# Seven-product pairs of steps in three feed-forward stages: four back-to-back pairs instead of three spaced ones, and two of a pair's weight sums made ahead in DRAM

## The reference

```
def swiglu(x, w_gu, w_down):
    gate, up = jnp.split(x @ w_gu, 2, axis=-1)       # w_gu: 1024 x 5632
    return (jax.nn.silu(gate) * up) @ w_down         # w_down: 2816 x 1024
# x = x + 0.5 * swiglu(rms_norm(x, g), w_gu, w_down)   four times; the fifth without the 0.5
```

## Time and profile before

| | |
|---|---|
| time, median of 3 runs | 1301.13 us (1301.01 to 1303.16) |
| the profiled execution | 1300.3 us, its span 1298.3 us |
| PE busy | 99% of the span |
| DVE, ACT busy | 72%, 62% |
| DMA | 265.83 MB, mean 205 GB/s |

### The profile page before, as it was taken

How to read it: one execution, slowest core, us unless ns; L and a number is a source line. 1 busy time by engine, 2 the same in 40 slices (tenths; PEclk the granted TensorE clock), 3 DMA queues, 4 the chain that set the end, 5 groups by cost and what they waited for, 6 DMA issues and landing times.

```text
span 1298.3 us, 17145 instructions
## 1 busy us (share of the span) xinstructions
PE 1281.1 (99%) x6976; PEld 1071.9 (83%) x6976; DVE 934.5 (72%) x1091; ACT 801.0 (62%) x1046; POOL 39.8 (3%) x61
## 2 busy tenths in 40 slices
PE   7999999999999999999999999999999999999998
PEld 6888888888988888888787888888888898788887
DVE  5887777777567877866353557678878798688785
ACT  7576658766556665684443466576556757755653
POOL 0000000000000000000000000001000000000000
PEclk9999999999999999999999999999999999999999
DMA  9987635432159778455444532498893534689761
GB/s 354 294 322 227 231 125 195 163 111 87 48 209 339 233 262 290 171 214 202 147 167 146 194 127 73 169 356 260 256 319 103 206 132 151 265 232 328 231 219 33
DMA packets 40206, 265.83 MB, mean 205 GB/s; under 512 B 4476, under 2 KB 6780, under 8 KB 9152
## 3 DMA queue, kind: packets, MB, share of 16 engines
q1 hardware_dynamic: 31056, 205.71, 42.4%
q0 software_dynamic: 7920, 56.37, 16.3%
q10 hardware_dynamic: 1152, 2.66, 0.6%
HBM read 263.67 MB, written 2.11 MB: 205 GB/s over the span
## 4 chain that ended last, share of the span: by engine, by line
PE 95%; ACT 2%; DVE 2%; issue 1%; DMA 0%; SPq 0%; ACTq 0%; DVEq 0%
PE ps L2451 25%; PE ps L2452 25%; PE ps L2453 25%; PE ps L2366 8%; PE ps L2602 1%; PE ps L2377 1%; PE ps L2492 1%; PE ps L2484 1%; PE ps L2497 1%; PE ps L485 1%; PE ps L2507 1%; PE ps L487 1%; PE ps L486 1%; ACT w_hi_part L584 1%; PE ps L2424 1%
## 5 line engine op out<-in xcount | busy, mean ns | idle before, releaser
L1492 DVE TENSOR_TENSOR w_lo_part<-w_raw,w_hi_part 128x2048 fp32r<-128x2048 f32 (+2 forms) x160 | 361.3, 2262 | 135.3 <-ACT w_hi_part L584 135.3
L584 ACT ACTIVATE w_hi_part<-w_raw 128x2048 fp32r<-128x2048 f32 (+2 forms) x159 | 301.4, 1896 | 156.2 <-PE ps L2453 135.1
L2451 PE MATMUL ps<-w_hi_part,x_hi 128*128 128x512 f32 (+1 forms) x800 | 312.3, 390 | 0.8 <-DVE w_lo_part L1492 0.5
L2453 PE MATMUL ps<-w_hi_part,x_lo 128*128 128x512 f32 (+1 forms) x800 | 305.5, 382 | 0.0
L2452 PE MATMUL ps<-w_lo_part,x_hi 128*128 128x512 f32 (+1 forms) x800 | 304.8, 381 | 0.0
L584 ACT ACTIVATE w_hi_part<-arena 128x2048 fp32r<-128x2048 f32 x72 | 138.1, 1918 | 97.4 <-PE ps L2453 93.1
L1492 DVE TENSOR_TENSOR w_lo_part<-arena,w_hi_part 128x2048 fp32r<-128x2048 f32 x72 | 164.6, 2288 | 39.4 <-ACT w_hi_part L584 39.4
L2451 PE MATMUL ps<-w_hi_part,h_hi_part 128*128 128x512 f32 x464 | 186.7, 402 | 0.1
L2453 PE MATMUL ps<-w_hi_part,h_lo_part 128*128 128x512 f32 x464 | 181.4, 391 | 0.0
L2452 PE MATMUL ps<-w_lo_part,h_hi_part 128*128 128x512 f32 x464 | 181.0, 390 | 0.0
L2453 PEld LDWEIGHTS ps<-w_hi_part,x_lo 128*128 128x128 f32 x800 | 150.4, 188 | 29.8
(11 more groups left out here) (443 smaller groups left out, 1555.9 us busy)
## 6 DMA issues: line engine op xcount, KB each, us to landing
w_raw<-in_tiles SPq DMA_DIRECT2D x155, 1024.0 KB, 4.9
arena<-in_tiles SPq DMA_DIRECT2D x36, 1024.0 KB, 6.4
arena<-in_tiles POOLq DMA_DIRECT2D x24, 1024.0 KB, 9.6
t<-in_tiles POOLq DMA_DIRECT2D x18, 1024.0 KB, 10.3
mem_kv<-in_tiles POOLq DMA_DIRECT2D x6, 1024.0 KB, 10.4
w_raw<-in_tiles SPq DMA_DIRECT2D x3, 512.0 KB, 5.9
arena<-in_w_ukv POOLq DMA_DIRECT2D x1, 1536.0 KB, 14.3
arena<-in_w_dkv POOLq DMA_DIRECT2D x1, 1280.0 KB, 8.7
```

The lines of the kernel that those rows point to most:

```text
L584: nc.scalar.activation(WH[:, n % RING, 0:w], source(n), ACT.Copy).then_inc(S["w_hi"], 1)
L1492: nc.vector.tensor_tensor(WL[:, n % RING, 0:w], source(n), WH[:, n % RING, 0:w], ALU.subtract).then_inc(S["w_split"], 1)
L2451: nc.tensor.matmul(o, a_hi, w_hi, start=start, stop=False, skip_group_check=True)
L2453: return nc.tensor.matmul(o, a_lo, w_hi, start=False, stop=stop, skip_group_check=True)
```

## The change

ffn1, ffn3 and ffn4 leave `PAIRED` for a new list `QUADS`; ffn0 and ffn2 stay. In a stage of QUADS steps 0, 1, 2 are plain, and pairs (3,4), (5,6), (7,8), (9,10) follow with nothing between them. A pair's order on PE is p5, m2, m1, p3, m6, d, m7, d, m4, with the downs of the pair before. The operands of m1, m2 and p3 come through the ring of raw tiles. T1 and T3 are made in a DRAM tensor `made_sums`: SP copies the first addend there (24 copies of 1 MB, DRAM to DRAM: one after the load of each of ain's tiles 4 to 11 for ffn1, two after each of mem's four loads for ffn3, one after every third load of ffn2 for ffn4), and POOL adds the second to it with accumulating DMAs (8 for each stage: ffn1's when all its 8 copies have landed, and each not before the split of one of ain's tiles 6 to 13; ffn3's during ffn2, ffn4's during in2). SP loads the finished sums into SBUF (TA twice, TC once). DVE still makes T2, in place; T4 is made by one accumulating DMA from POOL onto T2. ACT does the norm of such a stage ahead of its first two `w_hi`.

```diff
-PAIRED = ("ffn0", "ffn1", "ffn3", "ffn4")
+PAIRED = ("ffn0",)
+QUADS = ("ffn1", "ffn3", "ffn4")
+QUAD_STEPS = (3, 5, 7, 9)
+def quad_order():
+    order = [("g0", 0), ("g1", 0), ("g0", 1), ("g1", 1), ("d", 0), ("g0", 2), ("g1", 2)]
+    for s in QUAD_STEPS:
+        order += [("p5", s), ("m2", s), ("m1", s), ("p3", s), ("m6", s), ("d", s - 2), ("m7", s), ("d", s - 1), ("m4", s)]
+    return order + [("d", 10), ("d", 9)]
...
+            def copies_after(n):
+                t = n - tile0["ain"] - 4
+                if 0 <= t < 8:
+                    return range(t, t + 1)
+                t = n - tile0["mem"]
+                if 0 <= t < 4:
+                    return range(8 + 2 * t, 10 + 2 * t)
+                t = n - tile0["ffn2"] - 4
+                if 0 <= t < 24 and t % 3 == 0:
+                    return range(16 + t // 3, 17 + t // 3)
+                return ()
+            def copy_block(i):
+                q, k = divmod(i, 2)
+                name, s = QUADS[q // len(QUAD_STEPS)], QUAD_STEPS[q % len(QUAD_STEPS)]
+                t = stored0[name] + stored_at("g0", s + k)
+                sp.dma_start(made[q, k, :, :], d["tiles"][t, :, :], max_dma_last_dim=4 * TILE).then_inc(copied(name), 16)
+            def t_load(name, s, k):
+                dst, (sem, _) = ((TA[QUAD_STEPS.index(s) % 2], t1_loaded(name, s)), (TC, t3_loaded(name, s)))[k]
+                sp.dma_start(dst, made[quad_no(name, s), k, :, :]).then_inc(sem, 16)
...
                 sp.dma_start(RAW[:, r % RING, 0:w], d["tiles"][t, :, 0:w]).then_inc(w_loaded[r % RING], 16)
+                for c in copies_after(n):
+                    copy_block(c)
...
+                def quad_of_steps(s):
+                    if s == QUAD_STEPS[0]:
+                        pe.wait_ge(S["sums"], sum_no[name, "s_lo", 0])
+                    s_product("p5", s, 7, True, False)
+                    turn_pair(s - 1 if s == QUAD_STEPS[0] else s - 2)
+                    x_product("m2", s, 5, 0, 1, True, True)
+                    if s > QUAD_STEPS[0]:
+                        turn_pair(s - 1)
+                    x_product("m1", s, 4, 0, 0, True, False)
+                    pe.wait_ge(S["snap"], snaps_to(name, s, 1))
+                    s_product("p3", s, 7, False, True)
+                    pe.wait_ge(S["sums"], sum_no[name, "c11", s])
+                    s_product("m6", s, 4, False, False)
+                    down_half(s - 2, 0)
+                    down_half(s - 2, 1)
+                    pe.wait_ge(S["sums"], sum_no[name, "c12", s])
+                    s_product("m7", s, 4, False, False)
+                    down_half(s - 1, 0)
+                    down_half(s - 1, 1)
+                    if s == QUAD_STEPS[-1]:
+                        turn_pair(10)
+                    pe.wait_ge(S["sums"], sum_no[name, "c22", s])
+                    x_product("m4", s, 4, 1, 1, False, True)
...
+            def make_sums(name, paced):
+                pool.wait_ge(copied(name), 16 * (n_pairs + (3 if name == "ffn3" else 2) * len(QUAD_STEPS)))
+                for i, n in enumerate(paced):
+                    s, k = QUAD_STEPS[i // 2], i % 2
+                    pool.wait_ge(S["w_split"], n + 1)
+                    pool.dma_start(made[quad_no(name, s), k, :, :], stored(name, ("g0", "g1")[k], s + 1), accum_op=ALU.add,
+                                   max_dma_last_dim=4 * TILE).then_inc(S["base_loaded"], 16)
+            def t4_sums(name):
+                for s in QUAD_STEPS:
+                    split(name, "m6", s)
+                    pool.dma_start(TA[QUAD_STEPS.index(s) % 2], stored(name, "g1", s), accum_op=ALU.add).then_inc(t4_added(name, s)[0], 16)
...
             for s in PAIR_STEPS:
                 pair_sums("ffn0", s)
-            for s in PAIR_STEPS:
-                pair_sums("ffn1", s)
-            pool.wait_ge(S["tile_used"], unit_of["ffn1", "p3", PAIR_STEPS[-1]] + 1)
+            make_sums("ffn1", range(tile0["ain"] + 6, tile0["ain"] + 14))
+            t4_sums("ffn1")
...
+            make_sums("ffn3", range(tile0["ffn2"] + 2, tile0["ffn2"] + 26, 3))
...
+            pool.wait_ge(*made_all("ffn3"))
+            make_sums("ffn4", range(tile0["in2"] + 1, tile0["in2"] + 9))
+            t4_sums("ffn4")
```

More of the change, by code:

```diff
@@ L824, in paired_ffn, with quad_ffn, at, x_blocks @@
                 hidden_hi(10)
+                w_hi(ends[name] + 1)
+            def quad_ffn(f, name, first):
+                def at(kind, s):
+                    return unit_of[name, kind, s]
+                def x_blocks():
+                    act.wait_ge(S["act_ready"], 4 * version[name] + 4)
+                    for half in range(2):
+                        for k in range(4):
+                            last = nc.scalar.activation(AF[:, 2 * half:2 * half + 2, k, :], PS[:, half:4:2, k * P:(k + 1) * P],
+                                                        ACT.Copy, scale=gain(name, 4 * half + k))
+                    last.then_inc(S["x_blocks"], 1)
+                def s_hi():
+                    act.wait_ge(S["sums"], sum_no[name, "s", 0])
+                    nc.scalar.activation(SH[:, :, :, :], AF, ACT.Copy).then_inc(S["x_blocks"], 1)
+                def gate(s, tb):
+                    if tb == 0:
+                        act.wait_ge(S["gu_ps"], gu_no[name, s] + 1)
+                    else:
+                        act.wait_ge(S["tile_used"], at("g1", s) + 1)
+                    if s == 0 and tb == 0:
+                        act.wait_ge(S["norm_rs"], scale_no[name] + 1)
+                    if s == 1:
+                        act.wait_ge(S["h_raw"], TB * STEPS * f + tb + 1)
+                    nc.scalar.activation(SG[:, tb, :], bank(gu_bank(s, tb), CW), ACT.Silu,
+                                         scale=RSV[:, tb:tb + 1]).then_inc(S["sg_ready"], 1)
+                def snap(dst, b, kind, s):
+                    act.wait_ge(S["tile_used"], at(kind, s) + 1)
+                    if kind == "p5" and s > QUAD_STEPS[0]:
+                        act.wait_ge(S["h_raw"], hiddens_to(f, s - 1, 1))
+                    nc.scalar.activation(dst, bank(b), ACT.Copy).then_inc(S["snap"], 1)
+                def gate_of(block, s, which, tb):
+                    act.wait_ge(S["sums"], sum_no[name, which, s])
+                    nc.scalar.activation(block[:, 0:CW], block[:, 0:CW], ACT.Silu, scale=RSV[:, tb:tb + 1]).then_inc(S["sg_ready"], 1)
+                def gate_21(s):
+                    act.wait_ge(S["tile_used"], at("m4", s) + 1)
+                    nc.scalar.activation(SG[:, 1, :], bank(4, CW), ACT.Silu, scale=RSV[:, 1:2]).then_inc(S["sg_ready"], 1)
+                def hidden_hi(s):
+                    act.wait_ge(S["ht_ps"], turns_to(f, s))
+                    nc.scalar.activation(HH[:, 2 * (s % 2):2 * (s % 2) + 2, :], pairs(bank(6)), ACT.Copy).then_inc(S["h_hi"], 1)
+                for u in range(4):
+                    turned_hi(name, u)
+                first()
+                w_hi(at("g0", 1))
+                w_hi(at("g1", 1))
+                gate(0, 0)
+                gate(0, 1)
+                x_blocks()
+                hidden_hi(0)
+                w_hi(at("d", 0))
+                w_hi(at("g0", 2))
+                gate(1, 0)
+                gate(1, 1)
+                w_hi(at("g1", 2))
+                hidden_hi(1)
+                s_hi()
+                w_hi(at("p5", 3))
+                w_hi(at("m2", 3))
+                gate(2, 0)
+                gate(2, 1)
+                w_hi(at("m1", 3))
+                snap(P5F, 7, "p5", 3)
+                w_hi(at("p3", 3))
+                w_hi(at("m6", 3))
+                hidden_hi(2)
+                snap(C11F, 5, "m2", 3)
+                w_hi(at("d", 1))
+                w_hi(at("m7", 3))
+                snap(C12F, 7, "p3", 3)
+                gate_of(C11F, 3, "c11", 0)
+                w_hi(at("d", 2))
+                gate_of(C12F, 3, "c12", 0)
+                w_hi(at("m4", 3))
+                w_hi(at("p5", 5))
+                gate_of(P5F, 3, "c22", 1)
+                w_hi(at("m2", 5))
+                gate_21(3)
+                w_hi(at("m1", 5))
+                hidden_hi(3)
+                w_hi(at("p3", 5))
+                w_hi(at("m6", 5))
+                snap(P5F, 7, "p5", 5)
+                snap(C11F, 5, "m2", 5)
+                w_hi(at("d", 3))
+                snap(C12F, 7, "p3", 5)
+                hidden_hi(4)
+                w_hi(at("m7", 5))
+                gate_of(C11F, 5, "c11", 0)
+                w_hi(at("d", 4))
+                gate_of(C12F, 5, "c12", 0)
+                w_hi(at("m4", 5))
+                w_hi(at("p5", 7))
+                gate_of(P5F, 5, "c22", 1)
+                w_hi(at("m2", 7))
+                gate_21(5)
+                w_hi(at("m1", 7))
+                hidden_hi(5)
+                w_hi(at("p3", 7))
+                w_hi(at("m6", 7))
+                snap(P5F, 7, "p5", 7)
+                snap(C11F, 5, "m2", 7)
+                w_hi(at("d", 5))
```

(57 more changed lines are left out.)

274 lines of the change are left out of this document (247 added, 27 removed).

## The result

The changed kernel takes 1314.86 us (median of 6 runs, 1311.27 to 1317.37), the kernel before 1302.65 us in the same session (6 runs, 1301.01 to 1304.52). The ratio is 1.009, with a 95% interval from 1.0072 to 1.0108: slower by 0.9%, a forecast of 1305.4 inside its range, 9.5 us too low.

The account below looks back on a forecast made before the run. The prediction took PE's work, busy 99% of the span, as the bound. From 1300.3 us, -6.9 (matmuls) +0.5 (pair waits) +9.7 (solve stall) +1.0 (in2) gave 1304.6; 0.8 for the median gave 1305.4, range 1293.5 to 1323.

Parts of the forecast that it names:

- What PE loses and gains: In the three changed stages, fewer matmuls save PE 2.3 us each, 6.9 in all; waits in the pairs add 0.5.
- The mechanism of the stall: In the triangular solve, copies and sums delay raw tiles; ACT waits in order, holding copies PE needs: 9.7 us.
- Its size and its place: Stall of 9.7 us at out0 0, landing at 326.3 us; waits at mem 2 and mem 3 counted as the same lateness.
- The copy: DRAM to DRAM copy of 1 MB in ain and mem: 3.2 us of DMA engine work, bounds 2.44 and 4.5.
- The bias_rows row: Profile row at 884 to 889 us, nearest neighbour for the copy's price: 3.0 us of work over some 4.5 us.
- the prediction's formula at out0 0: In the solve, out0 0 lands at 235.9 + 16c + 8a, c per copy, a per sum; stall is that plus 2.8 less 319.4.
- rival B: DMAs partly hidden in the solve: copy between 2.5 and 3.1 us, stall 3 to 8 us, 1298 to 1303.5 us; chance 0.13.
- The accumulation into DRAM: Each 1 MB sum into DRAM takes 4.9 us of DMA engine work, as into SBUF, bounds 2.44 and 6.
- in2: In stage in2, sums starting with ring loads at the same split make in2 7 late: +1.0 us, between 0 and 2.5.
- A: DMAs hidden in the solve: ACT meets no late tile, only the gain is left, 1294.7 us; chance 0.34.
- C: Copy takes its clock time, 4.5 us: out0 0 lands at 347, stall of 30 us in the solve, 1326 us; chance 0.11.
- D: DVE becomes the bound in the changed stages: twelve pairs lose 1 us each, DMAs hidden, 1306.7 us; chance 0.04.

Follow-up runs that it names:

- e3: The changed kernel without any copies or sums in DRAM, T1 and T3 loaded as plain stored tiles: 1296.01 us, 0.9958 of the kernel before.
- e2: The changed kernel with ffn3's eight copies behind the loads of out0's four tiles instead of mem's: 1298.6 us, 0.9971 of the kernel before.
- e4: The changed kernel with ffn1's sums waiting for mem's tile 3 split and ffn4's sums in bin instead of in2: 1295.41 us, 0.9948 of before.
- e1: The changed kernel with ffn1's eight sums waiting for the split of mem's tile 3, all copies unmoved: 1298.64 us, 0.997 of the kernel before.
- e6: The changed kernel with ffn1's eight accumulations into DRAM replaced by plain copies of the same size and places: 1298.81 us, 0.9982 of before.

## Why the prediction was right, and where not

**What PE loses and gains: right.** Forecast -6.9 us with +0.5 of waits in the pairs, -6.4; measured -2.21 - 2.04 - 2.37 = -6.6. e3, with no DRAM work, has the same stages (177.54, 177.79, 177.56). T4's accumulation does end late for ACT (three waits in ffn1, of 3.3 us at 454.65 and up to 4.9), but PE doesn't wait for it here; that margin is thin, as the prediction said, and e2 and e4 overstep it by 0.7 to 1.0 us. Of the forecast's 0.5 us for waits the stages leave 0.3.

**ffn2 at 0: right** (207.39 against 207.35).

**The mechanism of the stall: right.** Full engines from the sums' start at 243.2 us (forecast 243.1) on, ACT behind a tile of w_raw, the triangular solve's copies behind the split, PE idle; parity of bytes between the queues while both have work, 8.39 to 8.93 MB; all taken back by e1, e2 and e6. One link was missing: at mem 2 the last copy is not ACT's but DVE's, behind DVE's own split, which costs 2.5 us more than ACT's (316.0 to 313.5). At out0 0, where the prediction looked, DVE's split stands behind that copy in the kernel before (321.36, the copy at 315.52), so there ACT's is the link.

**Its size and its place: the step that failed.** Forecast 9.7 us at out0 0, measured 15.1 at mem 2. The prediction called the waits at mem 2 and mem 3 "the same lateness, not more" and priced only the last tile. But the sums are all past before mem 2: up to its landing the engines have five loads, four copies and eight sums from 243.1 on. Even with the prediction's own prices, 243.1 + 12.2 + 12.8 + 38.1 + 2.4 = 308.6 (38.1 is 39.2 less the 1.1 done). ACT wanted it at 294.40, and could have it 2.0 us late, since DVE came to its split of mem 2 only at 298.35, 2.0 us after ACT's had ended (it was 310.81 - 0.84 - 294.40 = 15.6 late, for 13.6 at PE). That is 12 us where out0 0 gave 9.7. A tile in the middle can be the worst when what pushes it back ends before it; each tile needs its own sum.

**The copy: over-priced, 3.2 instead of 2.5 us.** In ain, with a full queue, the copies of 209.28 and 218.37 landed 12.6 and 13.3 us after issue, at 221.88 and 231.67: two loads and two copies in 9.8 us, 4.9 for a load and a copy together; less 2.44 for the load, 2.5. Windows of the kernel after, q1 alone, with that full queue and then behind it:

```profile
216.90:236.60 19.70, 19.70 (x110) 16.98 (x109) 14.79 (x30) 14.32 (x24) 0.00 (x0) 1.00 0.99 397
236.60:243.00 6.40, 6.40 (x30) 5.31 (x29) 6.13 (x11) 5.84 (x6) 0.00 (x0) 1.00 0.67 265
```

The eighth copy still lands at 242.9, since the ring's slots were free later than assumed and the queue ran dry in between (second row, a share of 0.67). So "the queue never runs dry" was wrong too, and the two errors cancelled. The bias_rows row was a poor neighbour: it reads one short line again and again. The Trainium skill, page "DMA: Bandwidth & Descriptors", section "Latency and other measured facts", gives 207 to 214 GB/s in each direction for copies between HBM tensors, measured with rows 512 KiB or a padded 4 MiB apart. The tiles here are contiguous blocks of 1 MB, and 2.5 us are 420 GB/s, so its figure doesn't carry over to these rows.

With the measured prices the prediction's formula at out0 0 gives 235.9 + 16 x 2.5 + 8 x 5.2 = 317.5, a stall of 0.9 us, but it holds only for a queue that is never empty. From the eighth copy's landing on, its count gives 242.9 + 17.1 + 20 + 41.6 - 1.1 + 2.4 = 322.9, a stall of 6.3 us, within rival B. So the forecast of 9.7 came near by luck: a copy too dear added 3.4 us, and looking two tiles too far on took off more. The same prices at mem 2 give 242.9 + 12.2 + 10 + 41.6 - 1.1 + 2.4 = 308.0, a stall of 11.6 us; it landed at 310.8.

**The accumulation into DRAM: right**, 5.2 us against 4.9. **in2**: +2.05 against +1.0, inside its bounds of 0 to 2.5, and the mechanism as told. **Not in the sum**: the clock's fall behind PE's idle time, 1.5 us, and the run itself: before's median was 2.4 us above its profiled execution here, not 0.8, and after's was 3.6 above.

From 1304.6 to the profiled 1311.27: stall +5.4, in2 +1.05, opening and end +0.5, changed stages -0.2: +6.8, where 6.7 is asked for.

*Rivals.* A (hidden) is what e3 and e4 are, 1296.01 and 1295.41 where it gave 1294.7; it fell for the change because copy and sum are 7.7 us for 1 MB together, above its point of 7.1, and mem 2 asks for more still (from 242.9 to 296.4, less five loads and a landing, and with the 1.1 us already done, there are 40 us for four copies and eight sums, which take 51.6). B (partly hidden, 1298 to 1303.5) is what the measured prices give at out0 0, and it fell because mem 2 was the tile that counts. C fell with the copy's price. D fell: DVE at 83% over the stage, PE busy for the whole of it.

## What to carry to other kernels

An engine's or a queue's mean share (0.34 here) says little on where extra transfers fit: count, for each tile that the path wants, all work that the DMA engines get before it, on every queue, and compare each with its own due time. Place off-path DMA work where no in-order engine stands on a load: the same work in another order (e4) made a change that lost 12 us win 7.

## What the runs showed of the hardware that was not expected

- A copy of 1 MB from DRAM to DRAM costs the DMA engines about what a load does, 2.5 us (landings in ain of the kernel after; 2.7 for loads and copies mixed by their share of the engines); an accumulation costs 5.2 us into DRAM and 4.9 into SBUF.
- Two queues that both had work shared by bytes (8.39 to 8.93 MB in 64 us), not by time: the queue with the dear transfers took 65.5% of the engines' time. In e2, where q1 was at times empty, q0 ran ahead (2.88 to 1.36 MB from 268 to 285 us).
- In PE's idle times of 4.6 and 8.1 us the granted clock fell to 0.50, the lower level, and stayed there for some 5 and 3 us after PE was busy again. Three of the eight profiled executions (e1, e2, e6) show a like fall (windows of 0.52 to 0.83) around the delta rule's small products, with PE busy. e1's instructions up to there are e4's, which has no such fall, so the kernel's text doesn't decide it; what does is not known.
